# A kernel's last step: the final norm of four row tiles, divided anew among ScalarE, GpSimd and VectorE

## The reference, cut to what matters here

```
y = _hierarchical_moe(h2, ...)            # each token: two experts, weights w1, w2
x = x + y.reshape(B, T, D)
return _rmsnorm(x, final_norm)            # x / sqrt(mean(x*x) + eps) * final_norm, per row
```

## Time and profile before

| | us |
|---|---|
| median of 3 runs | 1892.84 (1890.95 to 1894.92) |
| the profiled execution, its own time | 1894.98 |
| its span in the trace | 1892.9 |
| last expert row store issued (GpSimd) | 1863.99 |
| first tile's sum starts (VectorE) | 1873.48 |
| last tile's norm ends (VectorE) | 1889.89 |

### The profile page before, as it was taken

How to read it: one execution, slowest core, us unless ns; L and a number is a source line. 1 busy time by engine, 2 the same in 40 slices (tenths; PEclk the granted TensorE clock), 3 DMA queues, 4 the chain that set the end, 5 groups by cost and what they waited for, 6 DMA issues and landing times. The chain is left out here.

```text
span 1892.9 us, 21751 instructions
## 1 busy us (share of the span) xinstructions
PE 1785.1 (94%) x9049; PEld 1314.5 (69%) x9049; DVE 750.2 (40%) x1109; ACT 557.6 (29%) x859; POOL 233.5 (12%) x278
## 2 busy tenths in 40 slices
PE   7998999999999999998999999999999987999993
PEld 6877888888878787567888888878776673333331
DVE  4335322233365435645222232352347463223234
ACT  4325222222253124645322222252337410000001
POOL 3000000000001102420000000000004302323322
PEclk9979999999999998999999999999999987999997
DMA  7212343332232216402333332233230156999983
GB/s 228 90 45 67 90 110 89 92 107 89 91 116 89 89 47 196 139 23 67 90 96 104 89 102 98 89 120 99 71 112 24 53 220 268 368 382 398 380 325 146
DMA packets 179362, 260.20 MB, mean 137 GB/s; under 512 B 18889, under 2 KB 134793, under 8 KB 166993
## 3 DMA queue, kind: packets, MB, share of 16 engines
q1 hardware_dynamic: 155824, 204.66, 32.2%
q0 software_dynamic: 19424, 25.03, 4.2%
q10 hardware_dynamic: 4032, 29.36, 4.0%
HBM read 296.78 MB, written 29.40 MB: 172 GB/s over the span
## 5 line engine op out<-in xcount | busy, mean ns | idle before, releaser
L149 DVE TENSOR_TENSOR RING_R<-RING,RING_R 128x2048 fp32r<-128x2048 f32 (+1 forms) x110 | 250.2, 2277 | 655.3 <-ACT RING_R L146 655.3
L168 PE MATMUL PB<-RING_R,OPS_R 128*128 128x512 f32 (+1 forms) x1056 | 414.4, 392 | 9.4 <-DVE RING_R L149 4.3
L170 PE MATMUL PB<-RING_R,OPS_R 128*128 128x512 f32 (+1 forms) x1056 | 409.6, 388 | 0.0
L169 PE MATMUL PB<-RING_R,OPS_R 128*128 128x512 f32 (+1 forms) x1056 | 409.6, 388 | 0.0
L146 ACT ACTIVATE RING_R<-RING 128x2048 fp32r<-128x2048 f32 (+1 forms) x110 | 208.4, 1897 | 335.3 <-DMA RING<-in_ffn_w_down 137.8
L168 PE MATMUL PB<-OPS_R,RING_R 128*128 128x512 f32 (+1 forms) x736 | 281.9, 383 | 7.8 <-DVE OPS_R L275 7.8
L169 PE MATMUL PB<-OPS_R,RING_R 128*128 128x512 f32 (+1 forms) x736 | 281.4, 382 | 0.0
L170 PE MATMUL PB<-OPS_R,RING_R 128*128 128x512 f32 (+1 forms) x736 | 281.3, 382 | 0.0
L168 PEld LDWEIGHTS PB<-RING_R,OPS_R 128*128 128x128 f32 x1056 | 199.5, 189 | 52.8 <-issue 6.5
L170 PEld LDWEIGHTS PB<-RING_R,OPS_R 128*128 128x128 f32 x1056 | 199.3, 189 | 41.0
L169 PEld LDWEIGHTS PB<-RING_R,OPS_R 128*128 128x128 f32 x1056 | 199.7, 189 | 38.8
(11 more groups left out here) (358 smaller groups left out, 1899.3 us busy)
## 6 DMA issues: line engine op xcount, KB each, us to landing
RING<-in_ffn_w_gate SPq DMA_DIRECT2D x44, 512.0 KB, 4.0
RING<-in_ffn_w_up SPq DMA_DIRECT2D x44, 512.0 KB, 5.3
RING<-in_ffn_w_down SPq DMA_DIRECT2D x44, 512.0 KB, 4.0
RING<-in_w_expert_gate SPq DMA_DIRECT2D x16, 1024.0 KB, 8.3
RING<-in_w_expert_up SPq DMA_DIRECT2D x16, 1024.0 KB, 11.4
OPS<-in_w_expert_gate SPq DMA_DIRECT2D x16, 1024.0 KB, 11.2
OPS<-in_w_expert_up SPq DMA_DIRECT2D x16, 1024.0 KB, 13.7
Y<-in_w_expert_down ACTq DMA_DIRECT2D x14, 1024.0 KB, 9.7
```

What stands on the lines that cost most here:

```text
L149: nc.vector.tensor_tensor(RING_R[:, raw], RING[:, raw], RING_R[:, high].bitcast(fp32), ALU.subtract).then_inc(s_wlo, 1)
L168: nc.tensor.matmul(o, x[0], w[0], start=start, stop=False)
L169: nc.tensor.matmul(o, x[0], w[1], start=False, stop=False)
L170: return nc.tensor.matmul(o, x[1], w[0], start=False, stop=stop)
```

## The change

The norm of a tile is a product of three things: the rows, a factor per row and the weights per column. Before, one VectorE instruction does both products for each tile. Now, for the first three tiles, ScalarE multiplies by the row factor (`ACT.Copy` with a scale, X to Y), and GpSimd then multiplies Y in place by the weights (`tensor_tensor`, Y and GP in SBUF). The last tile is still done by VectorE in one instruction. VectorE computes all four reciprocals. Two semaphores are new: `rows_scaled` (ScalarE to GpSimd) and `last_rows_normed` (VectorE to SP). SP still issues the stores in the order of the tiles.

```diff
--- before.py
+++ after.py
@@ -2506,6 +2506,8 @@
         l_st = Sig("norm_stats", MT)
         l_r = Sig("norm_rstd", MT)
         l_y = Sig("norm_scaled", MT)
+        l_ya = sem("rows_scaled")
+        l_yd = sem("last_rows_normed")
         s_out = sem("out_stored")
         R1, R2 = [RING[:, i * MT * D:(i + 1) * MT * D].rearrange("p (m n) -> p m n", m=MT) for i in range(2)]
 
@@ -2529,17 +2531,20 @@
                 nc.vector.scalar_tensor_tensor(X[:, m, :], R2[:, m, :], w2_[:, m, :], X[:, m, :], ALU.mult, ALU.add
                                                ).then_inc(l_a.sem, 1)
 
-            def normed(m):
+            def inverse(m):
                 dve.wait_ge(*l_st.at(m + 1))
                 nc.vector.reciprocal(stat[:, 32 + m:33 + m], stat[:, 16 + m:17 + m]).then_inc(l_r.sem, 1)
+
+            def normed(m):
                 dve.wait_ge(*l_r.at(m + 1))
                 nc.vector.scalar_tensor_tensor(Y[:, m, :], X[:, m, :], stat[:, 32 + m:33 + m], GP[:, 1, :],
-                                               ALU.mult, ALU.mult).then_inc(l_y.sem, 1)
+                                               ALU.mult, ALU.mult).then_inc(l_yd, 1)
 
             summed(0)
             for m in range(1, MT):
                 summed(m)
-                normed(m - 1)
+                inverse(m - 1)
+            inverse(MT - 1)
             normed(MT - 1)
 
         def last_act(act):
@@ -2551,6 +2556,14 @@
                 act.wait_ge(*l_sq.at(m + 1))
                 nc.scalar.activation(stat[:, 16 + m:17 + m], stat[:, m:m + 1], ACT.Sqrt, bias=stat[:, 60:61],
                                      scale=1.0 / D).then_inc(l_st.sem, 1)
+                if m:
+                    act.wait_ge(*l_r.at(m))
+                    nc.scalar.activation(Y[:, m - 1, :], X[:, m - 1, :], ACT.Copy, scale=stat[:, 31 + m:32 + m]).then_inc(l_ya, 1)
+
+        def last_rows(pool):
+            for m in range(MT - 1):
+                pool.wait_ge(l_ya, m + 1)
+                nc.gpsimd.tensor_tensor(Y[:, m, :], Y[:, m, :], GP[:, 1, :], ALU.mult).then_inc(l_y.sem, 1)
 
         out_v = out[0].rearrange("(m p) n -> p m n", p=P)
         s_init = sem("init")
@@ -2578,7 +2591,10 @@
                 load_chunk(sp, n)
             moe_sync(sp)
             for m in range(MT):
-                sp.wait_ge(*l_y.at(m + 1))
+                if m < MT - 1:
+                    sp.wait_ge(*l_y.at(m + 1))
+                else:
+                    sp.wait_ge(l_yd, 1)
                 sp.dma_start(out_v[:, m, :], Y[:, m, :]).then_inc(s_out, 16)
             sp.wait_ge(s_out, 16 * MT)
 
@@ -2661,6 +2677,7 @@
                 pool.dma_start(h2_dram[m * P:(m + 1) * P, :], Y[:, m, :]).then_inc(s_h2, 16)
             moe_pool(pool)
             last_pool(pool)
+            last_rows(pool)
 
         @block.scalar
         def _(act):
```

## The result

The changed kernel takes 1903.52 us (median of 5 runs, 1901.15 to 1905.80), the kernel before 1893.29 us in the same comparison (1890.95 to 1894.92): 0.51% slower, 95% interval 0.40% to 0.62%. The forecast was +3.2 us, with a range up to 1898.9. The loss is about 10 us, three times the forecast.

A forecast was written before the change was run, and what follows sets the result against it. The end was taken as bound by a nearly gapless VectorE chain; 2.6 us saved there, but SBUF port waits and paired stores move the last landing from 1892.5 to 1895.7: 1892.84 + 3.2 = 1896.0 us, range 1892.9 to 1898.9.

The forecast's parts named there:

- the sum: Program's end: chain of VectorE, GpSimd and store times with VectorE first, last GpSimd product ending 1891.80, +3.2 us.
- the end of GpSimd's third product less 1888.6: Program's end: general formula for the change of time; the forecast has that product ending at 1891.80.
- The closing sentence: Prediction is wrong in kind if the last store waits for VectorE, or GpSimd's first product has an unseen delay; unsized.
- the first rival: Last tile's sum: GpSimd takes the SBUF port before VectorE; +5.2 us, 1898.0 us; chance 0.28.
- Who is first: Last tile's sum: VectorE starts at 1881.66, GpSimd at 1881.68, a tie within trace precision; VectorE assumed first.
- the 0.28: Chance given to GpSimd going first at the last tile's sum, +5.2 us.
- GpSimd's longer covered start: Last tile's sum: about 0.2 us of a waiting GpSimd product's start is covered, 0.15 for VectorE; reason for VectorE first.
- A held VectorE instruction: SBUF contention at the end: a waiting VectorE instruction ends 1.28 - 0.15 = 1.13 us after GpSimd's end.
- A held GpSimd product: SBUF contention at the end: a waiting GpSimd product ends 2.4 - 0.2 = 2.2 us after VectorE's end.
- the three rows: Earlier overlaps pricing contention: VectorE 2.45 us against 2.295, GpSimd 1.04 against 0.77, GpSimd 5.58 against at most 5.1.
- The pair of stores: Last two stores, issued together: the fourth lands 2.6 us plus 1.3 us of the third's data later, 3.9 us.
- Rival 3: Program's end: GpSimd and VectorE hardly block each other on SBUF; +0.7 us, 1893.5 us; chance 0.15.

The follow-up runs named there:

- e12: Changed kernel, GpSimd's three products replaced by memsets that read nothing, and GpSimd's drain at the end skipped: 1.0000 of the kernel before, tail 27.0 us.
- e1: Changed kernel with GpSimd's drain at the program's end skipped: 1.0021 of the kernel before, tail 29.7 us.
- e5: Changed kernel, GpSimd's first product also waiting for VectorE's second reciprocal, so VectorE goes first: 1.0045 of the kernel before, tail 34.5 us.
- e3: Kernel before plus one 128x1 GpSimd memset that waits for the last tile's norm: 1.0037 of the kernel before, tail 32.6 us.
- e6: Kernel before plus the 128x1 GpSimd memset waiting for the second tile's norm, 5.5 us earlier: one run, tail 27.2 us.
- e4: Changed kernel, GpSimd's three products replaced by 128x2560 memsets that read nothing, drain kept: one run, tail 31.7 us.
- e11: Changed kernel traced once more, nothing altered, to see which engine starts first: one run, tail 34.2 us.
- e2: Kernel before with GpSimd's drain at the program's end skipped: 1.0004 of the kernel before, tail 26.4 us.
- e13: Changed kernel, end drain kept, plus one GpSimd drain in the middle of the experts where GpSimd waits: 1.0021 of the kernel before, tail 29.4 us.
- e8: Changed kernel, GpSimd's products replaced by a multiply with constant 1.0 that reads one SBUF tensor: one run, tail 33.8 us.

## Why the prediction was wrong, point by point

**The account.** The tail grew from 26.0 to 36.5 us. The division of the work by itself makes +0.9 (e12). Products that read SBUF beside VectorE, VectorE first, +2.7 (e1 against e12: 29.7 against 27.0). GpSimd first instead, +2.0 (after against e5). The drain, +4.8 (e5 against e1, both with VectorE first). These four are steps from one trace to the next, so that their sum is the whole by construction and proves nothing; that each step is what its name says rests on e3 and e6 for the drain, on e4 for the read, on e5 and e11 for the order. Each is sure to about half a us, the first least of all: against e2, the other unchanged kernel without the drain, it is +0.5.

**The step that failed** is a term that was not in the sum: "the span ends" was tied to the last store's landing, in the sentence "In general the change of time is the end of GpSimd's third product less 1888.6". The sum has no price for what GpSimd does behind its last product. In its place the runs showed a drain: once GpSimd does the last work, the span ends 8.9 us behind GpSimd's last instruction plus 0.25, while the two stores need only 3.9. That is 9.2 less the stores' 3.9 and the barrier's 0.3, about 5 us more than the sum has (5.0 in SyncE's wait, 4.8 by e5 against e1). In the kernel before, GpSimd's work begins to cost time where the two meet, 25.74 + 0.3 - 9.2 = 16.8 us behind the first gather's start; e6's memset ends 18.0 us behind it (1883.43 less 1865.41), 1.2 us past that point, and its tail is 1.15 us longer. The trace of before held the row, a drain of 16.2 us that ended 6.6 us early, and none of the views that the prediction read shows work that is hidden at a barrier. The closing sentence named a delay on GpSimd that no row shows, and looked for it at the first product; it came behind the last one.

**The landing of the last store was forecast well.** With VectorE first: +3.2 forecast, +3.4 in e1 (29.16 less 25.74). With GpSimd first: +5.2 forecast as the first rival, +5.6 after. Of both, 0.4 to 0.6 us are the later start of the second tile's sum, which belongs to the execution and not to the change.

**Who is first** was called a tie, with the larger chance for VectorE. The first trace had GpSimd first, three others with the same work there (e1, e11, e13) VectorE, by 0.07 us each time where the sum had 0.02. One in four does not speak against the 0.28, and four traces cannot say more. The second reason given for VectorE, GpSimd's longer covered start, did not help it: in the first trace GpSimd led by 0.01 us and kept its length. The difference of 2 us between the two orders is confirmed by e5.

**The prices.** GpSimd's product 2.4 us: 2.35 measured. A held VectorE instruction ends 1.13 us after the other: 1.07 (1884.55 less 1883.48). A held GpSimd product ends 2.2 us after: 2.20 (1886.75 less 1884.55). One of the three rows that these prices were read from does not fit them, though: by the lengths at 512 and 1024 columns (1.275 and 2.35 us) a product of 2048 takes about 4.5 us, an estimate, and after the 2.1 us that VectorE had left it should have taken 6.4; it took 5.58. The prediction only noted that this was over 5.1. ScalarE's products 1.13: as forecast. VectorE's sums move up as forecast (e4: 1.30 us apart, last norm at its own length). The pair of stores 3.9 us: 3.94 (1893.06 to 1897.0). Rival 3 falls for this kernel; its sum holds for the form that only writes. The Trainium skill's rule (SBUF — State Buffer, "Who interferes with whom"), weighed in the prediction, is borne out by e4 and e5: whoever starts first keeps the port, and a GpSimd instruction that only writes does not interfere; e8 is a case in which "for the whole instruction" does not hold: VectorE ended 0.65 us before the GpSimd instruction that had held it. There the measurement decides.

## What to carry to other kernels

Before work is moved to an idle engine at the end of a program, look at what that engine still does behind its last instruction, up to the end barrier, though it is hidden now; here the program ends no earlier than 9.2 us behind GpSimd's last instruction, be it a memset of 0.1 us. And an idle engine is no free one when it reads SBUF beside VectorE instructions with two SBUF inputs: count the two as one engine, and count on the less lucky order, since the two starts lay within 0.1 us of each other here and it changed from trace to trace. If late work on GpSimd is wanted, a drain placed where GpSimd waits anyway takes the price from the end.

## What the runs showed of the hardware that was not expected

- A GpSimd drain takes time for DMAs that have long landed: 0.16 us with none since the program's start, 0.71 with 8 plain ones, 1.24 with 13 indirect, 2.19 with 49 plain, 8.68 with 104 indirect, 9.01 with the whole program's 153 (0.1 us of a memset included in the 0.16, 1.24, 8.68 and 9.01).
- A GpSimd multiply by a constant of 128x1024 took 2.74 us, longer than the two-input product's 2.35, and let a VectorE instruction with two SBUF inputs run beside its later part.
- A lead of 0.01 us (1881.13 against 1881.14) was enough to keep GpSimd at 2.35 us and to make VectorE's 1.28 us into 3.41.
